# Output product of the last two row tiles in two separate halves, the next stage's first weights split inside the attention loop, the query projection by halves

## Reference, cut to what matters

```python
for l in range(DEPTH):
    a, g, zc, q, k, v, za, qi, ki, wi = split(h @ w_in[l])
    y_conv = conformer_conv_branch(a, g, zc, ...)          # 512 columns
    y_attn = dsa_sparse_attention(...) * silu(za)          # 512 columns
    y = concatenate([y_conv, y_attn]) @ w_out[l]           # contraction over 1024 = conv 512 + attn 512
    h = layer_norm(ALPHA * h + y, ...)
# second model, one layer
z = rmsnorm(h) @ w_in_2        # q (512 columns), k and v (256), vin, u, gates ...
```

## Time and profile before

| | us |
|---|---|
| median of 3 runs | 1046.04 (1044.41 to 1047.38) |
| the profiled execution, its own time | 1047.51 |
| its span, first to last instruction | 1045.7 |
| PE busy | 993.5 (95%) |
| DVE busy | 653.0 (62%) |
| ACT busy | 582.4 (56%) |
| POOL busy | 198.7 (19%) |
| mean granted TensorE clock | 0.989 of full |

### The profile page before, as it was taken

The page is one execution under the profiler, slowest core; times in us unless marked ns, Lnnn a source line. Parts: engine busy times, 40 slices in busy tenths (PEclk is TensorE's granted clock), DMA queues, the critical chain, the costliest instruction groups (busy, mean ns, idle before and its releaser), DMA issues.

```text
span 1045.7 us, 16515 instructions
## 1 busy us (share of the span) xinstructions
PE 993.5 (95%) x6452; PEld 838.9 (80%) x6452; DVE 653.0 (62%) x1423; ACT 582.4 (56%) x948; POOL 198.7 (19%) x238
## 2 busy tenths in 40 slices
PE   6999999998999899999999899899999899999997
PEld 6998988885577799898888676787888778878885
DVE  3899999876573489999987554637522333332422
ACT  6585881657444458588165834644656565554331
POOL 0100771113120210067111311224200000000001
PEclk9999999998999999999999899999999999999999
DMA  8776874844203768477474521857777535466662
GB/s 294 184 181 172 213 182 122 185 98 122 41 1 94 182 160 192 122 175 187 122 181 102 160 56 41 217 146 182 181 196 211 117 81 139 104 147 135 170 152 81
DMA packets 23820, 152.35 MB, mean 146 GB/s; under 512 B 2864, under 2 KB 3376, under 8 KB 6848
## 3 DMA queue, kind: packets, MB, share of 16 engines
q0 software_dynamic: 9648, 68.75, 35.4%
q1 hardware_dynamic: 14096, 82.55, 22.1%
HBM read 149.20 MB, written 2.10 MB: 145 GB/s over the span
## 4 chain that ended last, share of the span: by engine, by line
PE 79%; ACT 10%; DVE 5%; DMA 4%; issue 2%; POOL 0%; POOLq 0%; SPq 0%; DVEq 0%; ACTq 0%
PE psum_B L1274 20%; PE psum_A L1274 15%; PE psum_A L1307 8%; PE psum_B L1307 8%; PE psum_A L1456 5%; DMA w_lo<-in_weights 3%; PE psum_C L1349 2%; PE psum_A L1667 2%; PE psum_B L1667 2%; ACT w_hi L640 2%; PE psum_B L1410 2%; ACT w_lo L641 2%; PE psum_B L1456 2%; ACT exps L761 1%; DMA w_raw<-in_weights 1%
## 5 line engine op out<-in xcount | busy, mean ns | idle before, releaser
L1752 DVE SCALAR_TENSOR_TENSOR conv_acc<-u,vec,conv_acc 128x528 f32<-128x528 f32 (+1 forms) x240 | 172.4, 756 | 3.2
L1073 POOL DMA_DIRECT2D w_lo<-in_weights x67 | 59.3, 886 | 577.2 <-ACT w_lo L641 551.0
L1274 PE MATMUL psum_B<-x_hi,w_hi 128*128 128x264 f32 (+3 forms) x480 | 134.8, 321 | 5.3 <-DVE mlp_lo L2199 3.6
L640 ACT ACTIVATE w_hi<-w_raw 128x2048 fp32r<-128x2048 f32 (+2 forms) x87 | 129.8, 1493 | 12.7 <-DMA w_raw<-in_weights 12.2
L1274 PE MATMUL psum_B<-x_lo,w_hi 128*128 128x264 f32 (+3 forms) x480 | 132.6, 317 | 0.0
L1274 PE MATMUL psum_B<-x_hi,w_lo 128*128 128x264 f32 (+3 forms) x480 | 132.2, 316 | 0.0
L641 ACT ACTIVATE w_lo<-w_raw 128x2048 fp32r<-128x2048 f32 (+2 forms) x87 | 129.2, 1485 | 0.0
L1274 PE MATMUL psum_A<-x_hi,w_hi 128*128 128x264 f32 (+2 forms) x528 | 125.4, 291 | 3.4 <-DMA w_lo<-in_weights 2.2
L1274 PE MATMUL psum_A<-x_hi,w_lo 128*128 128x264 f32 (+2 forms) x528 | 122.7, 287 | 0.0
L1274 PE MATMUL psum_A<-x_lo,w_hi 128*128 128x264 f32 (+2 forms) x528 | 122.7, 286 | 0.0
L1274 PEld LDWEIGHTS psum_A<-x_hi,w_hi 128*128 128x128 f32 x528 | 87.5, 188 | 7.5 <-issue 5.6
(11 more groups left out here) (362 smaller groups left out, 2120.1 us busy)
## 6 DMA issues: line engine op xcount, KB each, us to landing
w_raw<-in_weights SPq DMA_DIRECT2D x67, 1024.0 KB, 5.3
w_lo<-in_weights POOLq DMA_DIRECT2D x65, 1024.0 KB, 8.4
x_first<-in_x_t SPq DMA_DIRECT2D x4, 528.0 KB, 7.1
h<-in_x SPq DMA_DIRECT2D x1, 2048.0 KB, 10.8
out<-h SPq DMA_DIRECT2D x4, 512.0 KB, 2.6
post_ln_g<-in_post_ln_g SPq DMA_DIRECT2D x2, 512.0 KB, 8.7
post_ln_b<-in_post_ln_b SPq DMA_DIRECT2D x2, 512.0 KB, 10.6
w_raw<-in_weights SPq DMA_DIRECT2D x2, 288.0 KB, 5.4
```

The source lines that it names most:

```text
L640: act.activation(whi[n % RING][:, a:b], raw[n % RING][:, a:b], ACT.Copy)
L1073: pool.dma_start(wlo[n % RING][:, 0:width], io["weights"][n, :, 0:width], accum_op=ALU.add) \
L1274: mm = pe.matmul(ps[0:cols, i, 0:b - a], w[wp][:, kt, at:at + cols], x[xp][:, kt, a:b], start=(kt == 0 and wp + xp == 0), stop=(kt == KD - ...
L1752: got = dve.scalar_tensor_tensor(dst, src, w, dst, ALU.mult, ALU.add)
```

## The change

It has four parts.

1. **Output halves apart.** For tiles 3 and 4 each half product closes its own accumulation, takes its own bank and gets its own `residual` (conv halves with factor ALPHA and no `bn_stats`, attention halves with factor 1). Conv halves sit at items 25, 31, 33, 37 in layer 0 and 22, 25, 27, 29 in layer 1; attention half (0,3) at 35 and 30. Full products (1,0) and (1,1) of layer 0 move from items 22 and 25 to 21 and 23.
2. **Tail.** Layer 0: `turn_rows(0)` and `(1)` move into the loop (item 39); then attention half (1,3), `turn_rows(2)`, attention halves (0,4), (1,4). Layer 1: `turn_rows(1)`, attention half (1,3), `turn_rows(2)`, attention halves (0,4), (1,4). The queues of DVE, ACT and POOL follow.
3. **Next weights.** a0 is split at items 35 and 36 of layer 0, kv at 28 and 29 of layer 1; their loads start after conv half (0,4), those of g0 and q half 0 after conv half (1,4).
4. **Second model's start.** kv0, kv1, `turn_rows(3)`, kv2, q0 first half, `turn_rows(4)`, first halves of q1 and q2, kv3, second halves of q0, q1, q2, both halves of q3. ACT splits q half 1 between the copies of kv0 and kv1, vin half 1 after that of q0.

```diff
-KV_AND_Q = (("kv", 0), ("kv", 1), ("kv", 2), ("q", 0), ("kv", 3), ("q", 1), ("q", 2), ("q", 3))
...
-        blocks.append(((l, "wo", 1, 0), BLOCK, (l, "wo", 1, 3, "conv")))
+        blocks.append(((l, "wo", 1, 0), BLOCK, (l, "wo", 1, 4, "conv")))
...
 OUTPUT_AT = {
-    0: ((17, 0, 0, "A"), (19, 0, 1, "B"), (22, 1, 0, "A"), (25, 1, 1, "B"), (27, 0, 2, "A"), (29, 1, 2, "A"),
-        (35, 0, 3, "A")),
-    1: ((17, 0, 1, "A"), (19, 0, 2, "B"), (21, 1, 1, "A"), (23, 1, 2, "A"), (27, 0, 3, "A")),
+    0: ((17, 0, 0, "A", 1, None), (19, 0, 1, "B", 1, None), (21, 1, 0, "A", 1, None), (23, 1, 1, "B", 1, None),
+        (25, 0, 3, "A", 1, "conv"), (27, 0, 2, "A", 1, None), (29, 1, 2, "B", 1, None), (31, 0, 4, "A", 1, "conv"),
+        (33, 1, 3, "A", 1, "conv"), (35, 0, 3, "A", 1, "attn"), (37, 1, 4, "A", 1, "conv")),
+    1: ((17, 0, 1, "A", 1, None), (19, 0, 2, "B", 1, None), (21, 1, 1, "A", 1, None), (22, 0, 3, "B", 1, "conv"),
+        (23, 1, 2, "A", 1, None), (25, 0, 4, "A", 1, "conv"), (27, 1, 3, "A", 1, "conv"), (29, 1, 4, "A", 1, "conv"),
+        (30, 0, 3, "C", 0, "attn")),
 }
...
-OUTPUT_CONV_AT = {0: (37, 39), 1: (29, 31)}
-OUTPUT_BANK = (("A", 1), ("C", 0))
-INPUT_BANK = {0: ("D", "B", "D", "D", "C"), 1: (None, "D", "B", "D", "C")}
+INPUT_BANK = {0: ("D", "C", "D", "C", "D"), 1: (None, "D", "C", "D", "C")}
+KV_AND_Q = (("kv", 0), ("kv", 1), ("kv", 2), ("q", 0, 0), ("q", 1, 0), ("q", 2, 0), ("kv", 3),
+            ("q", 0, 1), ("q", 1, 1), ("q", 2, 1), ("q", 3, 0), ("q", 3, 1))
+KV_BANK = (("B", 0), ("A", 0), ("B", 0), ("B", 0))
+Q_BANK = (("A", 0), ("A", 1), ("B", 1), ("A", 0))
...
 SPLITS_AT = {
-    0: ((0, 1, ("zc", 2)), (2, 3, ("wo", 0, 0)), (5, 6, ("wo", 1, 0)), (12, 13, ("wo", 0, 1)), (17, 19, ("wo", 1, 1))),
-    1: ((0, 1, ("zc", 2)), (2, 3, ("wo", 0, 0)), (5, 6, ("wo", 1, 0)), (12, 13, ("wo", 0, 1)), (17, 17, ("wo", 1, 1))),
+    0: ((0, 1, ("zc", 2)), (2, 3, ("wo", 0, 0)), (5, 6, ("wo", 1, 0)), (12, 13, ("wo", 0, 1)), (17, 19, ("wo", 1, 1)),
+        (35, 36, ("next", "a", 0))),
+    1: ((0, 1, ("zc", 2)), (2, 3, ("wo", 0, 0)), (5, 6, ("wo", 1, 0)), (12, 13, ("wo", 0, 1)), (17, 17, ("wo", 1, 1)),
+        (28, 29, ("next", "kv", 0))),
 }
...
# ACT, behind the loop
-                split_hi(after, 0)
-                y_hi(l, "attn", 4)
-                split_hi(after, 1)
                 if l < DEPTH - 1:
                     x_hi(l, 0)
-                x_hi(l, 1)
-                x_hi(l, 2)
-                split_hi(after + 1)
-                if l < DEPTH - 1:
-                    x_hi(l, 3)
-                    x_hi(l, 4)
+                    x_hi(l, 1)
+                    y_hi(l, "attn", 4)
+                    split_hi(after + 1)
+                    for t in (2, 3, 4):
+                        x_hi(l, t)
                     split_hi(after + 2)
                 else:
+                    y_hi(l, "attn", 4)
+                    x_hi(l, 1)
+                    split_hi(after + 1)
+                    x_hi(l, 2)
                     squares(3, square)
-                    split_hi(after + 2)
...
-            for name, t in KV_AND_Q:
-                take_rows(name, t)
-                if (name, t) == ("kv", 1):
+            for name, t, *half in KV_AND_Q:
+                if name == "kv" or half == [1]:
+                    take_rows(name, t)
+                if (name, t) == ("kv", 0):
+                    split_hi(NUMBER[(2, "q", 1)])
+                elif (name, t) == ("kv", 1):
                     x_hi(DEPTH - 1, 3)
                     squares(4, square)
...
# PE
+            def output_rows(l, n, t, buf, bank_, part):
+
+                if part:
+                    use = (l, "wo", n, t, "conv") if part == "conv" else (l, "wo", n, t)
+                    ps = claim(use, buf, (bank_,))[:, 0, :]
+                    output_half(l, n, 0 if part == "conv" else 1, t, ps, True).then_inc(psum_full.mark(use), 1)
+                    return
...
-                ps = claim((l, "wo", 1, 3), "A", (0,))[:, 0, :]
-                output_half(l, 1, 0, 3, ps).then_inc(psum_full.mark((l, "wo", 1, 3, "conv")), 1)
-                if l < DEPTH - 1:
-                    turn_rows(l, 0)
-                turn_rows(l, 1)
-                output_attn(l, 0)
+                if l == DEPTH - 1:
+                    turn_rows(l, 1)
+                output_rows(l, 1, 3, "A", 0, "attn")
                 turn_rows(l, 2)
-                output_half(l, 1, 1, 3, ps).then_inc(psum_full.mark((l, "wo", 1, 3)), 1)
-                output_attn(l, 1)
+                output_rows(l, 0, 4, "A", 1, "attn")
+                output_rows(l, 1, 4, "B", 1, "attn")
...
+            def query_half(t, half):
+
+                use = (2, "q", t)
+                buf, at = Q_BANK[t]
+                ps = (bank[buf][:, at:at + 1, :] if half else claim(use, buf, (at,)))[:, 0, :]
+                w = [part[:, :].rearrange("p (k c) -> p k c", k=4) for part in weights(NUMBER[(2, "q", 0)] + half)]
+                for kk in range(4):
...
# DVE, in residual and behind the loop
+                if part == "attn":
+                    dve.wait_ge(dve_took.sem, dve_took.at((l, "wo", half, t, "conv")))
+                got = dve.scalar_tensor_tensor(dst, dst, 1.0 if part == "attn" else ALPHA, ps[0:n, 0, :], ALU.mult, ALU.add)
+                if part == "conv":
+                    got.then_inc(dve_took.mark(use), 1)
+                    return
...
                     second_input(1)
                     second_input(2)
                     x_lo(l, 1)
-                residual(l, 0, 4)
-                x_lo(l, 2)
-                residual(l, 1, 3)
+                residual(l, 1, 3, "attn")
                 aggregate(l, 3)
                 post_norm(l, 3)
-                residual(l, 1, 4)
+                x_lo(l, 2)
+                residual(l, 0, 4, "attn")
                 if l == DEPTH - 1:
                     second_input(3)
+                residual(l, 1, 4, "attn")
                 aggregate(l, 4)
                 post_norm(l, 4)
```

More of the change, by code:

```diff
@@ L115, in early_output @@
         for n in range(2):
[L116 to L118 removed]
+            uses.extend((l, "wo", n, t) for t in tiles if t < 3)
+        uses.extend((l, "wo", n, t, "conv") for n in range(2) for t in (3, 4))
+        uses.extend((l, "wo", n, t) for t in (3, 4) for n in range(2))
     def conv_input(l, c):
@@ L150, in weight_stream @@
         blocks.append(((l, "q", half), BLOCK, (l, "q", 3)))
-    uses.extend((l, *row) for row in KV_AND_Q)
+    uses.extend((l, name, t) for name in ("kv", "q") for t in range(4))
     for name in ("vin", "u", "gb"):
@@ L296, in attention_extras @@
             todo["pool"][i + 1].append(("input", t))
-    for part, i in enumerate(OUTPUT_CONV_AT[l]):
-        todo["pe"][i].append(("wo conv", part))
+    if l == 0:
+        todo["pe"][n - 1].extend([("rows", 0), ("rows", 1)])
     if l == 0:
@@ L1669, in branch @@
                 mm.then_inc(psum_full.mark(use), 1)
-            for name, t in KV_AND_Q:
+            def query_half(t, half):
[4 more added lines that the diff above has]
+                for kk in range(4):
+                    kt = 4 * half + kk
+                    for wp, xp in PASSES:
+                        mm = pe.matmul(ps, x[xp][:, kt, META + P * t:META + P * t + P], w[wp][:, kk, :],
+                                       start=(kt == 0 and wp + xp == 0), stop=(kt == KD - 1 and wp == 1))
+                if half:
+                    mm.then_inc(psum_full.mark(use), 1)
+            for name, t, *half in KV_AND_Q:
                 if name == "kv":
                     x_ready(1, t + 1)
-                    rows((2, "kv", t), NUMBER[(2, "kv", 0)], x, META + P * t, 1, 2 * P, 0, KD)
-                    if t in (1, 2):
-                        turn_rows(1, t + 2)
-                else:
-                    rows((2, "q", t), NUMBER[(2, "q", 0)], x, META + P * t, 2)
+                    buf, at = KV_BANK[t]
+                    rows((2, "kv", t), NUMBER[(2, "kv", 0)], x, META + P * t, 1, 2 * P, 0, KD, banks=(buf, (at,)))
+                    if t == 1:
+                        turn_rows(1, 3)
+                else:
+                    query_half(t, *half)
+                    if (t, *half) == (0, 0):
+                        turn_rows(1, 4)
+            turn["AB"] = 0
             for name in ("vin", "u", "gb"):
@@ L1930, in y_part, with residual @@
                         .then_inc(y_made.mark((l, part, t)), 1)
-            def residual(l, half, t):
-                use = (l, "wo", half, t)
+            def residual(l, half, t, part):
+                use = (l, "wo", half, t, "conv") if part == "conv" else (l, "wo", half, t)
                 n = SIZE[t]
```

55 lines of the change are left out of this document (21 added, 34 removed).

## The result

| | before | after |
|---|---|---|
| median, us | 1046.71 (4 runs, 1044.41 to 1049.08) | 1059.3 (4 runs, 1058.88 to 1061.51) |
| profiled execution, us | 1047.51 | 1061.51 |
| its span, us | 1045.7 | 1059.7 |
| mean granted clock | 0.989 | 0.982 |

The ratio is 1.0124, with a 95% interval of 1.0097 to 1.0152: slower by 12.6 us, where 4.95 were forecast, and above the end of the range (1055.0). In two later sets of rounds the same kernel stood 9.5 us (1057.77 against 1048.26, ratio 1.0071, 1.0044 to 1.0099) and 9.9 us (1057.31 against 1047.44, 1.0102, 1.0086 to 1.0118) above the kernel before. So the change costs some 10 us by the medians (7 to 13 by the ratios); the direction was right, and the forecast was half the size. The profiled execution of the table is the slowest of its four.

The account below looks back on a forecast made before the run. PE, busy 993.5 of 1045.7 us, was taken as the bound. Layer 0 (-0.8), layer 1's loop (+2.5) and its tail with the second model's start (+3.25) sum to +4.95 on 1046.04: 1051.0 us, range 1046.8 to 1055.0.

Parts of the forecast that it names:

- kv2: Second model's start: PE waits 3.9 us for `x_lo(3)`, 2.4 before, as ACT splits q half 1 first.
- vin: Second model's start: PE waits 2.7 us for half 1's `w_lo`, 0.35 before; 19.5 us from kv3's end.
- Turn 21: Layer 0, inside product (1,0): 2.9 us new wait for the last output block, net +1.4.
- Bank A1 in layer 0: Waits for the `residual` chain at items 27, 33, 35, 37: 3.55 us for 1.9 before, net +1.7.
- Layer 1's loop: Waits at items 25 and 27, turn 29, its product and the last values: 5.1 us for 2.6, +2.5.
- Transposes of tile 1: Layer 1's tail: `turn_rows(1)` waits 2.5 us for `second_input(1)`, or 2.1 at its lone price.
- The clock: Falls behind kv2's wait (1.75 us) and, once more, at layer 1's loop end (1.2 us on real matmuls).
- g0: Layer 0's end: block split in time, `w_lo` lands at 356.8; -0.8 us for all of layer 0.
- Early transfers: Rival: tail loads land sooner, shortening waits at kv2, vin and g0; 1047.2 us, chance 0.17.
- The clock doesn't fall: Rival: without two new falls 1048.0 us, chance 0.13; if those ahead of turn 17 vanish too, 1042.4, 0.05.
- Collision in layer 0: Rival: two raw loads fall on g0's `w_lo`, +2 us, ACT's split 0.5 to 1 late; 1053.5, chance 0.13.
- Theory A: From the experiments, not the prediction: waits as forecast, each new one followed by a half-clock stretch; forecast priced two.

Follow-up runs that it names:

- `after_third`: The changed kernel as it is, timed again in later rounds: 1057.31 us, ratio 1.0102 to the kernel before.
- `fill`: Changed kernel, nothing moved, unread transposes filling four PE waits (product (1,0), tile 1's transposes, kv2, vin): 1051.66 us, ratio 1.0046 to the kernel before.
- `fill_again`: Changed kernel with the same four waits filled as in `fill`, repeated in the rounds of `after_third`: 1051.41 us, ratio 1.0041 to the kernel before.
- `item22`: Changed kernel with layer 0's product (1,0) back at item 22: 1055.61 us, ratio 1.0074 to the kernel before.
- `fill_two`: Changed kernel with only the waits at kv2 and vin filled with unread transposes: 1057.81 us, ratio 1.0097 to the kernel before.
- `fill_loop`: Changed kernel with only the waits in product (1,0) and ahead of tile 1's transposes filled: 1056.32 us, ratio 1.0092 to the kernel before.
- `g0_early`: Changed kernel with layer 0's conv half (1,4) at item 35, attention half (0,3) at 37 in bank D0: 1053.77 us, ratio 1.0068 to the kernel before.
- `before_fill`: Kernel before, nothing moved, 21 unread transposes ahead of kv0 and of kv2: 1046.17 us, ratio 0.9991.
- `early_fill`: Kernel before, nothing moved, unread transposes in PE's waits ahead of turn 17 in both layers: 1047.45 us for 1048.26, ratio 0.9988.
- all edits: Changed kernel with reorderings at layer 0, layer 1's end and kv3, (wo,1,1) split earlier, q0's first half ahead of kv2: 1044.04 us, ratio 0.9973.

## Why the direction was right and the size wrong

**Waits, right within 0.4 us but for kv2 and vin.** Turn 21: 3.06 us for 2.9. Bank A1 in layer 0: 0.53, 1.24, 0.42 and 1.51, 3.7 for 3.55. Layer 1's loop: 1.23, 0.42, 0.39, 1.98 and 0.83, 4.85 for 5.1, with the squares' delay at turn 29 as described. Transposes of tile 1: 2.13; the forecast took 2.5 and named 2.1 for `second_input` at its lone price, which is what it cost (1.29 us in the chain). The pair still took 3.49 us: GpSimd's `x_lo` began only at 665.60, behind most of the first, so halving the pair's 3.53 us had been the wrong reading. kv2: 2.92 for 3.9; its mechanism (ScalarE splits q half 1 ahead of `x_hi(3)`) was right, the block landed earlier. vin: 3.2 for 2.7, with 19.9 us from kv3's end where 19.5 were worked out. That the 1.0 us too much and the 0.5 us too little partly cancel is luck.

**The clock, the step that failed.** "After a wait this long I take the clock to fall again, 1.75 us as before; and the 0.85 and 2.5 us at the loop's end ... to bring one more fall, of which 1.2 us meets real matmuls": a term of 2.95 us for two places. Measured in the profiled execution: 1.5 + 1.6 + 1.7 + 3.1 + 2.9 = 10.8 us at five (in `after_third` the first is missing). Two errors are in it. I asked of kv2 and of the loop's end whether the clock falls behind them, and not of turn 21, turn 29 and vin, whose waits of 2.9, 2.2 and 2.7 us stood in the same text; and I took the kernel before for the price, where such a stretch cost 1.8 us, while at kv2 and at vin it was twice as long. Runs bear out that the clock holds most of what was missed: `fill` and `fill_again` had none of those stretches and all of the waits, and stood 7.6 us (against an earlier set of rounds) and 5.9 us (in the same rounds) below the changed kernel. They don't bear out a fixed price per wait: `item22` had the waits of turn 29 and vin without a stretch, and `fill_two` and `fill_loop` gained nothing that can be told. With 4.95 - 2.95 = 2.0 us the forecast without these terms stands beside 4.0 (`fill_again`) and 5.1 (`fill`) measured.

The Trainium skill (TensorE: Matmul & The Clock Gate, HAM oscillation — how this bites in real kernels) describes a kernel in which each wait for a transfer makes the matmuls behind it start at the low clock, every time anew. The changed kernel agrees with it at vin in its three profiles and at turn 21 in two of three (kv2's wait, with the same effect, is for VectorE and not for a transfer); the waits for g0 here (2.2 us), for a0 and g0 before (2.2 and 2.8) and for vin in `item22` (3.0) had no such stretch, so a wait alone doesn't decide it.

**g0, wrong in sign.** The sum for layer 0 was -0.8 us and it is +3.05. 1.5 is the clock behind turn 21, and 0.4 stood there before turn 20. The rest is "its raw block is loaded after conv half (1,4) and split by ACT in time". It wasn't in time; the chain of the changed kernel:

```profile
334.61 9.04 DMA w_raw<-in_weights
...
343.67 1.92 ACT w_hi L645
345.59 1.81 ACT w_lo L646
...
347.75 12.68 DMA w_lo<-in_weights
...
360.56 3.15 PE psum_C L1278 x24
```

The raw load ran beside a0's `w_lo`, issued at 333.16 because a0 is now split inside the loop, and took 9.04 us where the median is 5.3. g0's `w_lo` then ran beside two raw loads (issued from 346.87 on) and took 12.68 us for 11.77. I had priced this collision as a rival (+2 us, chance 0.13) and left the raw block out of it. `g0_early` confirms the order of the two causes. a0 no longer waits for its weights, but 0.9 us for the `residual` of (0,4), whose bank it takes; that hadn't been seen either, and lies under the wait for g0.

**The rivals.** Early transfers: no, they were later than forecast. "The clock doesn't fall": the opposite. Collision in layer 0: yes, nearly at its price in sum, but most of it in the raw block and 0.9 us in `w_lo`. None had the case that happened, more falls than two. The range ended 9.0 us above the kernel before, below the distance of the medians in all three sets (9.5, 9.9, 12.6).

**Theory A as stated falls too.** A slow stretch is worth its length only where TensorE's own order sets the time. In the kernel before it stood in front of waits for transfers, and taking it away (`before_fill`, `early_fill`) lengthened those. Behind vin there is no such wait, which would explain why most of the loss stays in the changed kernel; this is argued and not shown, as `fill_two`, which filled kv2 and vin, gained nothing that can be told. What decides whether and how long TensorE runs slow behind a wait stays open.

## What to carry to other kernels

Price a new wait of two or three microseconds on the engine that bounds the kernel at twice its length, at every such wait alike, until traces show full clock behind it (here 13.3 us of new waits at five places went with 10.8 us of clock), and take more than one trace, as the stretches of one kernel differ from profile to profile. Before removing a wait or a slow stretch, look for the next transfer that the engine will reach earlier: of the 25.8 us that were summed up for all edits 15 came. And an operation split in halves to fill gaps shortens what lies over other loads: keep the count of matmuls between the release of a weight slot and the first use of its next block.
